# The last linear of a two-block kernel as seven products of half-size blocks

## The reference, cut to what matters

```python
def rms_norm(x, g):
    xf = x.astype(jnp.float32)
    var = jnp.mean(xf * xf, axis=-1, keepdims=True)
    return (xf * lax.rsqrt(var + RMS_EPS) * g.astype(jnp.float32)).astype(x.dtype)
...
        h = rms_norm(x, norm_ffn_pre[l])
        u = causal_dwconv(h @ w_up[l], conv_ffn_w[l])
        a, g = jnp.split(u, 2, axis=-1)
        f = (jax.nn.gelu(g, approximate=True) * a) @ w_down[l]
        x = x + rms_norm(f, norm_ffn_post[l])
```

## Time and profile before

| | |
|---|---|
| median of 3 runs | 1362.49 us (1362.31 to 1362.54) |
| the profiled execution's own time | 1362.46 us |
| its span | 1361.1 us |
| granted TensorE clock | 0.999 of full speed |
| PE busy | 1344.1 us (99%) |
| DVE, ACT, POOL busy | 767.6, 600.5, 4.0 us |

### The profile page before, as it was taken

One profiled execution on the slowest core, in us unless ns is written; L12 is line 12 of the kernel. 1 busy time (PEld: TensorE's weight loads), 2 busy tenths in 40 slices (PEclk: granted clock), 3 DMA queues, 4 the chain that ended last, 5 costly groups with the idle time before them and its releaser, 6 DMA issues.

```text
span 1361.1 us, 17268 instructions
## 1 busy us (share of the span) xinstructions
PE 1344.1 (99%) x6958; PEld 1117.8 (82%) x6958; DVE 767.6 (56%) x1088; ACT 600.5 (44%) x864; POOL 4.0 (0%) x11
## 2 busy tenths in 40 slices
PE   9999999999999999999999999999999999999998
PEld 7788877888888888889887777788998788888886
DVE  5779866776554443335525555345777666665232
ACT  5646778453333333233334545334634444443131
POOL 0000000000000000000000000000000000000000
PEclk9999999999999999999999999999999999999999
DMA  9734321423342223332231221223402322333431
GB/s 376 305 128 149 136 74 64 148 75 139 143 151 94 93 92 98 98 90 103 80 106 63 78 78 47 78 93 132 163 1 78 124 93 94 107 101 118 140 108 62
DMA packets 44526, 153.07 MB, mean 112 GB/s; under 512 B 5152, under 2 KB 7456, under 8 KB 43296
## 3 DMA queue, kind: packets, MB, share of 16 engines
q1 hardware_dynamic: 43568, 147.39, 31.0%
q0 software_dynamic: 880, 4.59, 1.0%
HBM read 146.97 MB, written 2.10 MB: 110 GB/s over the span
## 4 chain that ended last, share of the span: by engine, by line
PE 88%; DVE 7%; ACT 3%; issue 2%; DMA 0%; SPq 0%; ACTq 0%; DVEq 0%
PE banks L615 26%; PE banks L619 26%; PE banks L616 26%; DVE w_lo L1969 1%; PE banks L936 1%; ACT w_hi L1397 1%; PE banks L779 1%; PE banks L919 1%; PE banks L790 1%; PE banks L782 1%; DVE exact L2038 1%; PE banks L1227 1%; PE banks L1191 1%; PE banks L907 1%; PE banks L752 1%
## 5 line engine op out<-in xcount | busy, mean ns | idle before, releaser
L615 PE MATMUL banks<-h_hi,w_hi 128*128 128x512 f32 (+1 forms) x1248 | 469.9, 378 | 3.4 <-DVE w_lo L1969 2.9
L616 PE MATMUL banks<-h_hi,w_lo 128*128 128x512 f32 (+1 forms) x1248 | 465.2, 374 | 0.0
L619 PE MATMUL banks<-h_lo,w_hi 128*128 128x512 f32 (+1 forms) x1248 | 460.4, 375 | 0.8 <-DVE h_lo L2323 0.2
L1969 DVE TENSOR_TENSOR w_lo<-raw_w,w_hi 128x1024 fp32r<-128x1024 f32 (+2 forms) x215 | 250.9, 1169 | 283.1 <-ACT w_hi L1397 281.7
L1397 ACT ACTIVATE w_hi<-raw_w 128x1024 fp32r<-128x1024 f32 (+2 forms) x215 | 216.9, 1011 | 236.5 <-PE banks L619 219.1
L615 PEld LDWEIGHTS banks<-h_hi,w_hi 128*128 128x128 f32 x1248 | 234.9, 188 | 51.2 <-issue 6.1
L616 PEld LDWEIGHTS banks<-h_hi,w_lo 128*128 128x128 f32 x1248 | 235.0, 188 | 40.4
L619 PEld LDWEIGHTS banks<-h_lo,w_hi 128*128 128x128 f32 x1248 | 231.4, 188 | 44.6 <-DVE h_lo L2323 1.7
L615 PE MATMUL banks<-a_hi,w_hi 128*128 128x512 f32 (+1 forms) x198 | 72.5, 366 | 0.0
L619 PE MATMUL banks<-a_lo,w_hi 128*128 128x512 f32 (+1 forms) x198 | 72.4, 365 | 0.0
L616 PE MATMUL banks<-a_hi,w_lo 128*128 128x512 f32 (+1 forms) x198 | 72.3, 365 | 0.0
(11 more groups left out here) (336 smaller groups left out, 1685.3 us busy)
## 6 DMA issues: line engine op xcount, KB each, us to landing
raw_w<-in_w_ffn_up SPq DMA_DIRECT2D x44, 512.0 KB, 3.3
raw_w<-in_w_up SPq DMA_DIRECT2D x44, 512.0 KB, 3.6
raw_w<-in_ada_rows SPq DMA_DIRECT2D x24, 512.0 KB, 3.7
raw_w<-in_w_down SPq DMA_DIRECT2D x22, 512.0 KB, 3.6
early<-in_ada_turned SPq DMA_DIRECT2D x8, 1024.0 KB, 17.8
raw_w<-in_w_gates SPq DMA_DIRECT2D x16, 512.0 KB, 3.2
raw_w<-in_w_ffn_down SPq DMA_DIRECT2D x16, 448.0 KB, 3.2
raw_w<-in_w_conv SPq DMA_DIRECT2D x12, 512.0 KB, 3.2
```

The costliest lines, as they stand in the source:

```text
L615: e.matmul(dst, lhs_hi, rhs_hi, start=first, stop=False)
L616: e.matmul(dst, lhs_lo, rhs_hi, start=False, stop=False)
L619: return e.matmul(dst, lhs_hi, rhs_lo, start=False, stop=last)
L1969: e.tensor_tensor(lo[:, 0:n], raw[:, i % RAW, 0:n], hi[:, 0:n].bitcast(F32), ALU.subtract).then_inc(s_lo, 1)
```

## The change

The four quarters of the activations (rows of blocks 0 to 10 or 11 to 21, tokens 0 to 255 or 256 to 511) and the four quarters of the weights are combined by sums and differences, and seven products of quarters give the four quarters of the result.

- **Matmuls.** Seven products, each of 11 chunks x 2 token groups x 3 = 66 matmuls. A product has six weight tiles, five of 1024 columns and one of 512, so 42 tiles instead of 22, with 12 (or 6) matmuls for each instead of 24.
- **Sums of weights.** Product 1 and product 6 take a quarter of the weights as it is. The other five take sums or a difference. Four are made by POOL with transfers from memory to memory, 24 copies and 24 that add to their destination, from the first product of the first block's feed-forward on. The difference is made by loading two quarters (2.9 MB each) into the memory of `a2_hi` and `a2_lo` when `up2` has begun, by six subtractions on POOL and six transfers back. SP waits for all of them before it loads the first tile of `down2`, ACT before the first `split_hi`.
- **Differences of activations.** In the first eleven steps of `up2` the split is left out and one transpose of `x` put in. In the last eleven the step makes the inputs of products 0 and 1 with one more DVE subtraction, and splits those. The inputs of products 2 to 6 are split in `down2`, two products ahead of PE; three of these products need a DVE subtraction first.
- **Results.** Two banks per product. Products 2 and 3 add up in the banks of 0 and 1 once ACT has copied these to memory. DVE joins products by additions and subtractions. The token groups come in the order 2, 3, 0, 1; groups 0 and 1 need the last product.
- **The transfers that turn `x`** stand between loads of `up2` instead of `down2`.

```diff
-            for n in range(FC - RESIDENT):
...
+            for n in range(PRODUCTS * PER_PRODUCT - RESIDENT):
+                p, part = divmod(n, PER_PRODUCT)
+                chunks = range(2 * part, min(2 * part + 2, HC))
                 e.wait_ge(s_lo, W["down2"] + n + 1)
...
+                for j in chunks:
+                    inputs_of(p, j)
+                    for i in range(2):
+                        done = token_products(p, j, i)
...
+                done.then_inc(s_used, 1)
             e.wait_ge(s_lo, N_TILES)
...
+            for i in range(2):
+                for j in range(2 * (PER_PRODUCT - RESIDENT), HC):
+                    done = token_products(PRODUCTS - 1, j, i)
                 done.then_inc(s_y2, 1)
```

ACT in `down2`:

```diff
+            prepare(W["down2"] + 4)
+            for n in range(PER_PRODUCT * (PRODUCTS - 1)):
+                p, i = divmod(n, PER_PRODUCT)
+                prepare(W["down2"] + n + 4)
+                if p + 2 < PRODUCTS:
+                    high_part(p + 2, i)
+                if i == PER_PRODUCT - 1:
+                    if p == 0:
+                        copy_product(0, Y2_PRODUCT_0, 1)
...
             prepare(N_TILES)
```

DVE in `up2` and `down2`:

```diff
-                low(W["up2"] + (f + 9 if f < 3 else 2 * f + 6))
+                e.tensor_tensor(a2[:, f, :], u, y, ALU.mult).then_inc(s_up2_act.sem, 1)
+                if f >= HC:
+                    two_halves = u.rearrange("p (n q) -> p n q", n=2)
+                    e.wait_ge(*s_up2_act.at(act2_count(f)))
+                    e.tensor_tensor(two_halves, a2[:, f:f + 1, HALVES[1]].to_broadcast([P, 2, HALF]),
+                                    a2[:, f - HC, :].rearrange("p (n q) -> p n q", n=2), ALU.subtract).then_inc(s_up2_act.sem, 1)
...
+            for n in range(PER_PRODUCT * (PRODUCTS - 1)):
+                p, i = divmod(n, PER_PRODUCT)
+                if p + 2 in DIFFERENCES:
+                    difference(p + 2, i)
+                low(W["down2"] + n + 4)
+                if p + 2 < PRODUCTS:
+                    low_part(p + 2, i)
+                if i == PER_PRODUCT - 1:
+                    for half in range(2):
+                        if p == 3:
+                            join(Y2_PRODUCT_0, 3, half, "add", s_y2_copied.at(half + 1))
...
+            low(N_TILES)
...
+            for n, t in enumerate(Y2_ORDER):
+                if n >= 2:
+                    join(Y2_PRODUCT_4, 6, n - 2, "add", s_y2_joined.at(n + 3))
+                    join(Y2_PRODUCT_5, 6, n - 2, "less", s_y2_copied.at(n + 5))
```

POOL:

```diff
+            e.wait_ge(s_up_act, 1)
+            for p, (one, other) in SUMMED.items():
+                for i in range(PER_PRODUCT):
+                    part = slice(i * SLOT, min((i + 1) * SLOT, HC * T))
+                    moved(e.dma_start(down2_sums[p - 1, :, part], io["w_down2"][one, :, part]))
+                    e.wait_ge(*s_w_moved.at(16 * moves))
+                    moved(e.dma_start(down2_sums[p - 1, :, part], io["w_down2"][other, :, part], accum_op=ALU.add))
+            e.wait_ge(*s_up2_act.at(1))
+            moved(e.dma_start(w_late[:, :], io["w_down2"][3, :, :]))
+            moved(e.dma_start(w_early[:, :], io["w_down2"][0, :, :]))
...
+                e.tensor_tensor(w_late[:, part], w_late[:, part], w_early[:, part], ALU.subtract).then_inc(s_w_apart.sem, 1)
```

More of the change, by code:

```diff
@@ L169, in load_order @@
         l.block("up2", "w_up2", FC + f)
-    for t in range(FC):
-        l.wide("down2", "w_down2", t)
+    for p in range(PRODUCTS):
+        w = io["w_down2"][PLAIN[p], :, :] if p in PLAIN else io["down2_sums"][max(p - 1, 0), :, :]
+        for i in range(PER_PRODUCT):
+            first, beyond = i * SLOT, min((i + 1) * SLOT, HC * T)
+            l.tile("down2", w[:, first:beyond], beyond - first, 2 * i, (beyond - first) // T)
     return l
@@ L1351, in tensor_program @@
             turn = (turn + 2 * FC) % 6
-            y2_banks = ([turn, (turn + 1) % 6, *NORM_BANKS], [(turn + n) % 6 for n in range(2, 6)])
-            def token_products(n, j, t):
-                g, k = 2 * n // FC, (2 * n + j) % FC
-                (hi, lo), tok, w = kept_at(W["down2"] + n)[0], slice(t * P, (t + 1) * P), slice(j * T, (j + 1) * T)
-                b = y2_banks[g][t]
-                if k == 0:
-                    free(b)
-                return product(bank[b][:, :], a2_hi[:, k, tok], a2_lo[:, k, tok], hi[:, w], lo[:, w], k == 0, k == FC - 1)
@@ L1366, in tensor_program @@
[L1366 to L1376 removed]
+            y2_pairs = pairs_of_down2(turn)
@@ new lines, in token_products @@
+            def token_products(p, j, i):
+                (hi, lo), w = kept_at(W["down2"] + PER_PRODUCT * p + j // 2)[0], slice(j % 2 * T, (j % 2 + 1) * T)
+                tok, goes_on = slice(i * P, (i + 1) * P), p in (2, 3)
+                b = y2_pairs[p][i]
+                if j == 0:
+                    if goes_on:
+                        e.wait_ge(*s_y2_copied.at(2 * (p - 2) + i + 1))
+                    elif p == PRODUCTS - 1:
+                        e.wait_ge(*s_y2_joined.at(5 + i))
+                    else:
+                        free(b)
+                first, last = j == 0 and not goes_on, j == HC - 1
+                e.matmul(bank[b][:, :], a2_hi[:, j, p % 2, tok], hi[:, w], start=first, stop=False, skip_group_check=True)
+                e.matmul(bank[b][:, :], a2_lo[:, j, p % 2, tok], hi[:, w], start=False, stop=False, skip_group_check=True)
+                return e.matmul(bank[b][:, :], a2_hi[:, j, p % 2, tok], lo[:, w], start=False, stop=last, skip_group_check=True)
@@ L1951, in scalar_program, with copy_product @@
-            prepare(N_TILES)
-            for t in range(TT):
-                e.wait_ge(s_y2, TT + t)
-                y2_square(t, 1)
-                e.wait_ge(s_y2_bias, 1)
-                e.wait_ge(s_y2_sq, TT + t + 1)
+            y2_pairs = pairs_of_down2(turn)
+            def copy_product(p, place, first):
+                for i in range(2):
+                    e.wait_ge(*y2_product(p, i))
+                    if first == 1:
+                        e.wait_ge(s_x_moved, 16 * TT * TT)
+                    e.activation(part_of_y2(place, i), bank[y2_pairs[p][i]][:, :], ACT.Copy).then_inc(s_y2_copied.sem, 1)
@@ new lines, in join @@
+            def join(place, p, i, op, known):
+                e.wait_ge(*known)
+                e.wait_ge(*y2_product(p, i))
+                dst, product_of = part_of_y2(place, i), bank[y2_pairs[p][i]][:, :]
+                if op == "from":
+                    e.tensor_tensor(dst, product_of, dst, ALU.subtract).then_inc(s_y2_joined.sem, 1)
+                elif op == "less":
+                    e.tensor_tensor(dst, dst, product_of, ALU.subtract).then_inc(s_y2_joined.sem, 1)
+                else:
+                    e.tensor_tensor(dst, product_of, dst, ALU.add).then_inc(s_y2_joined.sem, 1)
@@ L2816, in sync_program @@
                 for a in range(0, TT, 2):
-                    beyond = loads.tile_load[W["down2"] + 8 + 2 * q + a // 2]
+                    beyond = loads.tile_load[W["up2"] + 26 + 2 * q + a // 2]
                     load(at, beyond)
```

214 lines of the change are left out of this document (146 added, 68 removed).

## The result

| | before | changed kernel |
|---|---|---|
| median of 20 runs | 1362.54 us (1362.16 to 1362.90) | 1364.49 us (1361.48 to 1368.93) |
| ratio to before, 95% interval | | 1.0017 (1.0010 to 1.0024) |
| the profiled execution: time, span | 1362.46, 1361.1 us | 1365.21, 1363.9 us |

The prediction was 1356.0 with a range up to 1363.5. The changed kernel is not faster; it is 1.9 us slower, which lies within the 0.2% that the prediction called no change. The measured time lies above the range. Its runs also spread over 7.5 us, those of before over 0.7.

What follows compares the result with a forecast made beforehand. PE, busy 99% of the span, was taken to bound the kernel. -15.0 + 3.5 + 2.2 + 2.7 = -6.6 us, so 1362.5 - 6.6 = 1355.9, stated as 1356.0, range 1352.5 to 1363.5.

Steps and rivals of the forecast that it cites:

- The matmuls: Down projection: 462 matmuls instead of 528, 66 fewer at 0.2267 us each, -15.0 us if PE is fed.
- The hand-over: Up to down projection: PE waits for the third tile, behind ACT's last split and table load and a DVE subtraction, +3.5 us.
- Work beside each tile: Down projection: DVE needs 2.37 of PE's 2.72 us per tile in products 0, 1 and 4; tile-by-tile walk gives 0.
- rival B: Down projection: DVE cannot keep PE's pace; 1363.1 us, or 1358.7 with smaller gaps; chance 0.14.
- The last loads: Before the last 42 matmuls: tile 40 loads only once a place is free, so PE waits, +2.2 us.
- The end: After the last matmul: the last token groups queue on DVE, 3.3 us each or 4.5 with two joins, +2.7 us.
- rival C: In `up2`: POOL's six subtractions block DVE, costing 0 to 8 us, 2.5 taken, so 1358.5; chance 0.08.
- The memory sums: From 292.8 to 1029.7: 24 pairs of transfers with 30.7 us for each pair, counted as covered.
- Covered edits: Transposes of `x`, differences in steps 11 to 21, turning transfers, memory sums and two large loads: no term in the sum.
- rival A: First block's up projection: adding transfers delay weight tiles beyond 5.6 us to spare, up to 24 times; 1389 at 7 us; chance 0.12.
- The two large loads: The two 2.9 MB loads before ACT's wait in step 11: some 25 to 40 us, with 120 us available.
- below 1359.8: Times faster by more than 0.2%: the forecast, rivals D (more gain) and C, half of B; 0.76, lowered to 0.73.

Runs made afterwards that it cites:

- e10: e3 with only ScalarE's table load moved from ahead of the down projection's third tile to product 3: 1354.39 us, 0.9944.
- e1: Changed kernel without the 48 memory-to-memory transfers, plain quarters loaded instead of sums (values wrong): 1357.97 us, 0.9960.
- e3: Changed kernel with the sums started after the last product of the first up projection instead of after the first: 1357.39 us, 0.9958.
- e5: Changed kernel with later sums, third tile split right behind the last convolution, table load moved to product 3, inputs of products 2 to 6 prepared three tiles later: 1354.57 us.
- e12: e3 with the first eight sum transfers issued early, one per step, in the gap after row and tiles have landed: 1357.54 us, 0.9963.
- e13: e3 with the first eight sum transfers issued early, one per step, at the moment row and tiles are issued: 1358.97 us, 0.9979.
- e2: Changed kernel with the 24 adding transfers made plain copies of the same size and place, sums not made: 1363.43 us, 1.0000.
- e8: Changed kernel with the sums started after product 10 of the first up projection, where steps load two tiles and no row: 1357.06 us, 0.9961.
- e14: e3 with fifteen sum transfers issued early, two per step, one adding and one copying, together with row and tiles: 1363.66 us, 1.0014.

## Why the prediction was wrong, by its own steps

**The matmuls: right.** 66 fewer, still 0.2267 apart: -15.0.

**The hand-over: the wait right, its sequel missing.** 3.3 us idle, 3.5 by starts, for +3.5, in the place and by the chain that was named. The sum left out that the clock falls behind this wait, 1.7 us. e10 shows it apart.

**Work beside each tile: right.** No wait of PE between the two named ones, so the walk's 0 holds and rival B is false.

**The last loads: right**, 2.2 us idle for +2.2, and 2.5 by starts with the matmuls just behind; the clock stayed up here, though it fell behind 2.3 to 3.0 us at this place in e1, e3, e5, e10 and e12.

**The end: right.** 8.0 - 5.2 = 2.8 for +2.7, with DVE's 3.3 and 4.5 per group.

**POOL's subtractions (rival C): the blocking right, the price 0.** Timeline of DVE beside them:

```profile
1061.72 2.87 DVE L2796 TENSOR_TENSOR a<-normed,exact 128x512 f32<-128x512 f32 x1 [0.70 <-ACT exact L1998]
1064.52 0.70 DVE L2781 STREAM_TRANSPOSE x_turned<-x_res 128x512 f32<-128x512 f32 x1
1065.14 6.62 DVE L2064 TENSOR_TENSOR w_lo<-raw_w,w_hi 128x1024 fp32r<-128x1024 f32 x2
```

0.69 became 2.87, and two low parts took 6.62 us instead of 2.36. That agrees with the Trainium skill (SBUF — State Buffer, "Who interferes with whom"), by which the two engines lock each other out for whole instructions; the transpose and the convolutions' 1.52 for two were not stretched. DVE's idle time and PE's lead took it: 223 matmuls in that window, as many as ever.

**The memory sums: this step failed.** Under "Covered edits" they cost 0, and rival A, which is what happened, had a chance of 0.12 and a condition that was wrong in two ways. The sign of it that the prediction named is there: PE reaches the down projection 7.3 us later than 1236.2. First, it weighed each adding transfer against 5.6 us to spare, as if each step had that anew. The 5.6 is PE's lead, there once. What is renewed is only the 1.63 us for which ACT waits for PE, and that row stood in the earlier trace rows beside the one that was used. A loop of loads that is late by more than that falls behind a little in each step: seven row issues gave 10.6 us of lag. The first wait follows from this. The low part of the step's first tile was ready at 343.1 (341.89 + 1.23), 7.0 us later than the kernel before had it (334.90 + 1.22), and PE needed it at 341.9 (320.1 and two steps of 10.88): 1.2 us late, as measured. Of the 7.0 us the row's issue had brought 4.4 (333.64 against 329.25) and the loads of that step 2.6, so no load was late by 5.6 of itself. Second, the price was X less 5.6, for each transfer, with X the time of an adding transfer. That time is 5.5 us in the gap and 9.4 beside the loads (e12, e13), so the rule would give nothing or 24 x 3.8 = 91 us; measured are 8.4. And the rival looked at adding alone. A single adding transfer is indeed the worse one (e13), but e2 shows that copies in a dense stream lose 4.7 of the 8.5 us as well: the median load of a tile took 5.2 us to land beside them, 5.5 beside the sums and 3.3 without.

That the share of DMA time is high is not the cause: e3 and e8 have the same or more without loss, e12 has none and e13 a lag with equal traffic. The rule of the Trainium skill that the prediction cited (DMA: Bandwidth & Descriptors, "Queues, rings and completion order"), engines that serve their queues in turn, agrees with loads that are slower beside another queue's transfers.

**Other covered edits.** The wait that is gone from `up2`, a gain of 1.1 us, was in no term. The two large loads landed 11.1 and 18.5 us after their issue, well under the 25 to 40 that were allowed. And the chances named for "below 1359.8" add up to 0.81 (0.58 + 0.08 + 0.08 + 0.07), not to 0.76; the forecast of the time does not use them.

**The sum again,** by starts of matmuls: -15.0 + 7.3 (8.4 less the 1.1 on the way) + 3.5 + 1.7 + 2.5 + 2.8 = +2.8, and +2.8 is measured for the span. With the sums out of the way the prediction's 1355.9 plus the clock's 1.7 is 1357.6, and e3 measured 1357.4, e1 1358.0. That is closer than the terms deserve, since the 1.1 us gained in `up2` and 0.3 more at the last loads are in neither; with both it would be 1356.8.

**Open.** What part of a load's delay comes from reads and what from writes was not separated, nor why one adding transfer at the loads lengthened a turn by 1.5 us in one step and by 3.0 in another. Nor was it settled when the clock falls. It fell behind every wait of 3.3 us or more that was looked at. Shorter ones went either way: at the last group it stayed up behind 2.2 and 2.3 us in the changed kernel, in e2 and in e8 and fell behind 2.3 in e3 and e10; in the first up projection it stayed up behind 1.8 us in e14 and fell behind 1.9 in e2.

## What to carry to other kernels

Before traffic is put beside a stretch of loads, find the loop that the loads form through the engines that free their places, and read its idle time in one turn: that is what may be spent per step, while the lead of the busiest engine can be spent once. Then choose the moment before the amount: steps that load no row (e8), or the gap behind a landing (e12), took the same bytes for nothing. Where a transfer must stand beside the loads, one that copies did far less harm here than one that adds. And price a stall of 3 us on PE with the slow matmuls that follow it: removing 1.4 us of one gave 2.9 in the trace. A short stall is no safe one, as e2 shows.

## What the runs showed of the hardware that was not expected

- A copy of 512 KB within memory took 3.8 us from issue to landing in the gap between loads, one that adds 5.5 (e12); beside a row and two tiles 6.7 and 9.4 (e13). In the changed kernel the copies look slower than the adding transfers (7.2 and 5.8 in the median), but nearly all of them are issued 0.5 us behind an adding one in the same queue.
- One adding transfer beside a row and two tiles, all issued together, moved the second tile's high part from 326.25 (in the gap, e12) to 329.51 (e13), 3 us, with DMA engines busy for about half of the time (0.48 from 300 to 350). One copy in that place moved it from 315.37 to 315.62, which is about how much later this run was anyway.
- Matmuls behind a wait of 3.3 us or more ran at 1.2 GHz, 0.43 us apart, for some seven to fourteen starts, which cost 1.5 to 3.0 us. The start of the slow stretch varies: in the changed kernel it begins with the first matmul behind the wait, in e8 and e14 some six matmuls later.
- A POOL subtraction of 128x1024 floats took 2.42 us, twice DVE's 1.2, and kept DVE's own subtractions out meanwhile.
